# Inverse of the delta rule's triangles: 32x32 and 64x64 tiles in the doubling steps, and a semaphore of its own for each scratch load

## The reference, cut to what matters

```python
lmat = jnp.where(strict, jnp.einsum('bhncd,bhnsd->bhncs', k_beta, k) * decay, 0.0)
tmat = lax.linalg.triangular_solve(eye + lmat, eye, left_side=True, lower=True)
u_c = jnp.einsum('bhncs,bhnsd->bhncd', tmat, v_beta)
```

## Time and profile before

| | |
|---|---|
| median of 3 runs | 2074.65 us (2069.03 to 2075.73) |
| the profiled execution | 2070.47 us |
| its span, first to last instruction | 2068.9 us |
| TensorE busy | 98% |
| VectorE, ScalarE, GpSimd busy | 45%, 36%, 4% |
| mean granted clock of TensorE | 0.991 |

### The profile page before, as it was taken

One profiled execution on the slowest core, in us unless ns is written; L12 is line 12 of the kernel. 1 busy time (PEld: TensorE's weight loads), 2 busy tenths in 40 slices (PEclk: granted clock), 3 DMA queues, 4 the chain that ended last, 5 costly groups with the idle time before them and its releaser, 6 DMA issues.

```text
span 2068.9 us, 33700 instructions
## 1 busy us (share of the span) xinstructions
PE 2021.4 (98%) x12540; PEld 1806.5 (87%) x12540; DVE 922.9 (45%) x2325; ACT 738.9 (36%) x2211; POOL 90.6 (4%) x115
## 2 busy tenths in 40 slices
PE   5999999999999999999999999999999999999996
PEld 5888899999999999999999988888888888888885
DVE  6333344556455455545556454322223534344332
ACT  5422224235252433525335252423224322223333
POOL 4000000000000000000000000000000000000000
PEclk8999999999999999999999999999999999999998
DMA  6133332234133241332323233343345444345222
GB/s 222 43 106 110 114 126 90 68 103 117 41 114 85 83 116 53 104 92 95 97 83 100 78 111 87 113 134 115 106 134 206 138 132 132 120 143 204 87 76 81
DMA packets 229516, 225.55 MB, mean 109 GB/s; under 512 B 33681, under 2 KB 214890, under 8 KB 228746
## 3 DMA queue, kind: packets, MB, share of 16 engines
q1 hardware_dynamic: 167090, 180.10, 27.0%
q10 hardware_dynamic: 55944, 22.63, 4.4%
q0 software_dynamic: 6368, 21.14, 3.1%
HBM read 199.65 MB, written 25.30 MB: 109 GB/s over the span
## 4 chain that ended last, share of the span: by engine, by line
PE 93%; DMA 3%; DVE 1%; ACT 1%; issue 1%; ACTq 0%; POOL 0%; SPq 0%; DVEq 0%
PE pj L518 80%; PE pg L518 10%; DMA st<-inverse_scratch 3%; PE pt L518 2%; PE pt L665 1%; PE pg L761 0%; PE pg L818 0%; DVE fst L1235 0%; POOL xl L1708 0%; ACTq L996 0%; DMA prow<-in_dn_norm_w 0%; ACT wh L859 0%; DVE res L1688 0%; DVE xl L1241 0%; ACTq L995 0%
## 5 line engine op out<-in xcount | busy, mean ns | idle before, releaser
L518 PE MATMUL pj<-xh,wh 128*128 128x264 f32 (+2 forms) x2688 | 739.2, 329 | 3.0 <-DVE wl L1210 3.0
L518 PE MATMUL pj<-xl,wh 128*128 128x264 f32 (+2 forms) x2688 | 719.8, 322 | 0.0
L518 PE MATMUL pj<-xh,wl 128*128 128x264 f32 (+2 forms) x2688 | 718.2, 322 | 0.0
L1210 DVE TENSOR_TENSOR wl<-raw,wh 128x256 fp32r<-128x256 f32 x896 | 346.3, 424 | 609.6 <-ACT wh L859 607.8
L518 PEld LDWEIGHTS pj<-xh,wh 128*128 128x128 f32 x2688 | 448.3, 190 | 46.9 <-issue 3.6
L518 PEld LDWEIGHTS pj<-xh,wl 128*128 128x128 f32 x2688 | 448.4, 190 | 38.0
L518 PEld LDWEIGHTS pj<-xl,wh 128*128 128x128 f32 x2688 | 448.2, 189 | 37.5 <-issue 1.0
L859 ACT ACTIVATE wh<-raw 128x256 fp32r<-128x256 f32 x896 | 306.3, 407 | 63.0 <-issue 42.7
L859 ACT ACTIVATE wh<-rawb 128x256 fp32r<-128x256 f32 x288 | 97.8, 406 | 182.2 <-PE pj L518 181.2
L518 PE MATMUL pj<-yl,wh 128*128 128x512 f32 x384 | 149.5, 389 | 0.0
L518 PE MATMUL pj<-yh,wl 128*128 128x512 f32 x384 | 149.5, 389 | 0.0
(11 more groups left out here) (210 smaller groups left out, 1719.5 us busy)
## 6 DMA issues: line engine op xcount, KB each, us to landing
raw<-in_w_in SPq DMA_DIRECT2D x112, 1024.0 KB, 6.3
rawb<-in_w_dn_out SPq DMA_DIRECT2D x16, 1024.0 KB, 6.1
rawb<-in_w_o SPq DMA_DIRECT2D x12, 1024.0 KB, 5.4
gates_scratch<-stg ACTq DMA_DIRECT2D x32, 256.0 KB, 2.1
rawb<-in_w_pool_out SPq DMA_DIRECT2D x8, 1024.0 KB, 5.5
gst<-gates_scratch POOLq DMA_DIRECT2D x32, 256.0 KB, 3.1
yraw<-branch_scratch SPq DMA_DIRECT2D x1, 5632.0 KB, 22.7
xt<-in_x SPq DMA_DIRECT2D x4, 1024.0 KB, 6.9
```

Of the source, the lines that this page charges most:

```text
L518: return pe.matmul(dst, lhs, rhs, start=start, stop=stop)
L1210: tt(wl[:, j, 2 * q:2 * q + 2, :], raw[:, 2 * par + h, 2 * q:2 * q + 2, c * P:(c + 1) * P], wh[:, j, 2 * q:2 * q + 2, :].bitcast(F32), ALU ...
```

## The change

The two lower levels no longer load whole slots. At L0 every 32x32 block on the diagonal of `mk` is its own product with the 16 columns of `tm` that belong to its upper half, written to the same 32 partitions: 4 for each slot. At L0+1 T takes three such products for each slot and comes first, Y takes four with 16 columns of weights. The second level uses 32x32 tiles (two for each slot in X and Y, one in T), and L0+4 a 64x64 tile. The masks are gone: X of the first level is scaled by a column `odd` that is 1 on rows 16 to 31 of each 32 and 0 elsewhere, the second level is copied from the right partitions. `xm`, `xm5` and `xm6` are three parts of `dec` that don't overlap, and nothing clears them. Where a block was zero, VectorE writes the negated product instead of subtracting. `tm` and the two loads of `st` get a semaphore each, and L0+1 waits for `st`. Four steps get an `alone()`.

```diff
@@ the column that replaces the masks
-    for i, size in enumerate((BS, 2 * BS)):
...
+    c[:, CODD] = s // BS % 2
@@ views of dec
-        xm = dec
+        xm = dec[:, 0:SLOTS * BS].rearrange("p (i c) -> p i c", c=BS)
+        xm5 = dec[:, 128:128 + SLOTS * 2 * BS].rearrange("p (i c) -> p i c", c=2 * BS)
+        xm6 = dec[:, 384:384 + SLOTS * LOWC].rearrange("p (i c) -> p i c", c=LOWC)
+        QUARTERS = [slice(32 * b, 32 * b + 32) for b in range(4)]
+        PAIRED = [(QUARTERS[0], QUARTERS[1]), (QUARTERS[2], QUARTERS[3])]
@@ TensorE
                 if m == L0:
-                    wait(inv_loaded, 48, 48)
-                    pe.wait_ge(masks_loaded, 16)
+                    wait(tm_loaded, 16, 16)
                     wait(qk_ready, 2, 2)
                     alone()
                     for i in range(SLOTS):
-                        mm = product(pg[0][:, LOWC * i:LOWC * (i + 1)].rearrange("p (b c) -> p b c", c=BS),
-                                     slot(mk, i), halves(slot(tm, i), BS, 0), True, True)
+                        for q in QUARTERS:
+                            mm = product(pg[0][q, BS * i:BS * (i + 1)], slot(mk, i)[q, q], slot(tm, i)[q, q.start:q.start + BS], True, True)
                     mm.then_inc(x_mm, 1)
                 if m == L0 + 1:
-                    wait(x_ready, 3, 1)
+                    wait(st_loaded, 32, 32)
+                    wait(x_ready, 4, 1)
+                    alone()
...
+                        for q in QUARTERS[0:3]:
+                            mm = product(pg[2][q, BS * i:BS * (i + 1)], slot(st, i)[q, q], xm[q, i, :], True, True)
+                    mm.then_inc(t_mm, 1)
...
+                        for q in QUARTERS:
+                            mm = product(pg[1][q.start:q.start + BS, BS * i:BS * (i + 1)], xm[q, i, :], slot(st, i)[q, q.start + BS:q.stop],
+                                         True, True)
                     mm.then_inc(y_mm, 1)
                 if m == L0 + 2:
                     wait(t_ready, 2, 1)
+                    alone()
...
+                        for first, second in PAIRED:
+                            mm = product(pg[0][second, 2 * BS * i:2 * BS * (i + 1)], slot(mk, i)[first, second], slot(tm, i)[first, first],
+                                         True, True)
                 if m == L0 + 3:
...
+                        mm = product(pg[2][second, 2 * BS * i:2 * BS * (i + 1)], slot(st, i)[second, second], xm5[second, i, :], True, True)
...
+                            mm = product(pg[1][first, 2 * BS * i:2 * BS * (i + 1)], xm5[second, i, :], slot(st, i)[second, second], True, True)
                 if m == L0 + 4:
...
-                        mm = product(pg[0][:, LOWC * i:LOWC * (i + 1)], slot(mk, i), slot(tm, i)[:, 0:LOWC], True, True)
+                        mm = product(pg[0][LOWC:P, LOWC * i:LOWC * (i + 1)], slot(mk, i)[0:LOWC, LOWC:P], slot(tm, i)[0:LOWC, 0:LOWC], True, True)
@@ ScalarE
-                    act.dma_start(slots(tm), full_rows(inv_d[1])).then_inc(inv_loaded, 16)
-                    act.dma_start(slots(st), full_rows(inv_d[0])).then_inc(inv_loaded, 16)
+                    act.dma_start(slots(tm), full_rows(inv_d[1])).then_inc(tm_loaded, 16)
+                    act.dma_start(slots(st), full_rows(inv_d[0])).then_inc(st_loaded, 16)
@@ VectorE
-                        dve.wait_ge(masks_loaded, 16)
-                        wait(xm_zeroed, 1, 1)
-                    tt(each(xm, BS << lv, 0), low(pg[0]).rearrange("p i (b c) -> p i b c", c=BS << lv), mask(lv), ALU.mult).then_inc(x_ready, 1)
+                if m == L0:
+                    wait(x_mm, 3, 1)
+                    dve.tensor_scalar(xm, by_slot(pg[0], BS), odd, None, ALU.mult).then_inc(x_ready, 1)
                 if m == L0 + 1:
                     wait(t_mm, 2, 1)
...
+                    for q in QUARTERS[0:3]:
+                        part = slots(tm)[q, :, q.start:q.start + BS]
+                        ins = tt(part, part, by_slot(pg[2], BS)[q], ALU.subtract)
+                    ins.then_inc(t_ready, 1)
+                    wait(y_mm, 3, 1)
+                    for q in QUARTERS:
...
+                if m == L0 + 2:
+                    wait(x_mm, 3, 2)
+                    for first, second in PAIRED:
+                        dve.tensor_copy(xm5[second], by_slot(pg[0], 2 * BS)[second]).then_inc(x_ready, 1)
@@ GpSimd
-            pool.dma_start(lvm[:, :, :], consts[:, CLEV:CZERO].rearrange("p (l c) -> p l c", l=2)).then_inc(masks_loaded, 16)
-                pool.wait_ge(qk_ready, 2 * d + 2)
-                pool.sem_inc(pool_gate, 1)
-                pool.memset(xm[:, 0:XC], 0.0).then_inc(xm_zeroed, 1)
```

More of the change, by code:

```diff
@@ L691, in delta @@
                     mm.then_inc(x_mm, 1)
                 if m == L0 + 3:
-                    wait(x_ready, 3, 2)
+                    wait(x_ready, 4, 3)
                     wait(s_ready, 3, 1)
+                    alone()
+                    first, second = PAIRED[0]
                     for i in range(SLOTS):
-                        mm = product(pg[1][:, LOWC * i:LOWC * (i + 1)].rearrange("p (b c) -> p b c", c=2 * BS),
-                                     slot(xm, i), halves(slot(st, i), 2 * BS, 1), True, True)
+                        mm = product(pg[2][second, 2 * BS * i:2 * BS * (i + 1)], slot(st, i)[second, second], xm5[second, i, :], True, True)
@@ L698, in delta @@
+                    mm.then_inc(t_mm, 1)
+                    for i in range(SLOTS):
+                        for first, second in PAIRED:
+                            mm = product(pg[1][first, 2 * BS * i:2 * BS * (i + 1)], xm5[second, i, :], slot(st, i)[second, second], True, True)
                     mm.then_inc(y_mm, 1)
-                    for i in range(SLOTS):
-                        mm = product(pg[2][:, 2 * BS * i:2 * BS * (i + 1)], slot(st, i), slot(xm, i)[:, 0:2 * BS], True, True)
-                    mm.then_inc(t_mm, 1)
@@ L1443, in delta @@
                         dve.tensor_copy(wtr, wblk.rearrange("p a i -> p i a")).then_inc(w_turned, 1)
[L1445 to L1451, removed]
-                    return lvm[:, level, :].unsqueeze(1).broadcast_to([P, SLOTS, LOWC]).rearrange("p i (b c) -> p i b c", c=BS << level)
@@ L1467, in delta @@
+                if m == L0 + 2:
+                    wait(x_mm, 3, 2)
+                    for first, second in PAIRED:
+                        dve.tensor_copy(xm5[second], by_slot(pg[0], 2 * BS)[second]).then_inc(x_ready, 1)
                 if m == L0 + 3:
                     wait(t_mm, 2, 2)
-                    part = slots(tm)[32:64, :, 0:32]
-                    tt(part, part, pg[2][32:64, 0:32 * SLOTS].rearrange("p (i c) -> p i c", c=32), ALU.subtract).then_inc(t_ready, 1)
-                    for b in range(2):
-                        rows = slice(64 * b, 64 * b + 32)
-                        part = slots(st)[rows, :, 64 * b + 32:64 * b + 64]
-                        ins = tt(part, part, low(pg[1])[rows, :, 32 * b:32 * b + 32], ALU.subtract)
+                    first, second = PAIRED[0]
+                    part = slots(tm)[second, :, first]
+                    dve.tensor_scalar(part, by_slot(pg[2], 2 * BS)[second], -1.0, None, ALU.mult).then_inc(t_ready, 1)
+                    wait(y_mm, 3, 2)
+                    for first, second in PAIRED:
+                        part = slots(st)[first, :, second]
+                        ins = dve.tensor_scalar(part, by_slot(pg[1], 2 * BS)[first], -1.0, None, ALU.mult)
@@ L1483, in delta @@
                     wait(y_mm, 3, 3)
[L1484 to L1485 removed]
+                    dve.tensor_scalar(slots(st)[0:LOWC, :, LOWC:P], by_slot(pg[1], LOWC)[0:LOWC], -1.0, None, ALU.mult).then_inc(s_ready, 1)
                 if R0 <= m < O0:
```

54 lines of the change are left out of this document (19 added, 35 removed).

## The result

The changed kernel takes **2000.62 us** (median of 4 runs, 2000.11 to 2001.15), against 2071.84 for the kernel before in the same comparison: ratio 0.9657, 95% interval 0.9641 to 0.9673. Its profiled execution took 2000.11 us, 70.4 less than the one of before. I had forecast 2062 with a range from 2030 to 2086, so the forecast failed, and on the cautious side: the time lies nearest to the rival of the tiles that work side by side (1985).

What follows compares the result with a forecast made beforehand. The prediction took TensorE, busy 98%, to bound the kernel: 2070.5 - 9.4 (wait at L0) - 1 (units and shapes) + 0 (clock) = 2060 us, forecast as 2062 for a median, range 2030 to 2086.

Steps and rivals of the forecast that it cites:

- the rival of the tiles that work side by side: Rival for the five steps of the inverse: four units share one time, -74 us, giving 1985 us; chance 0.05.
- What bounds the kernel, and the wait at L0: TensorE, busy 98%, sets the end; L0 waiting for `tm` alone removes its gap in each pair, -9.4 us.
- The number of units: L0 to L0+4: more but smaller two-multiply units, 53 ns each once ready ones run out; sum -0.82 us a pair.
- the array's pace: Rival: units run at 31 ns for 32 columns and 25 for 16 throughout, giving 2034 us; chance 0.20.
- A sum of -0.1 us a pair: Units and changes of tile shape together in the inverse's steps, -1 us in all.
- Changes of shape: Switching tile shape around the bursts of the inverse costs 0.2 us in and out, +0.7 us a pair.
- VectorE: Its changed updates and copies cost nothing; uncovered, a late answer at L0+1 or L0+3 costs up to 1 us a pair.
- The clock: Falls of TensorE's granted clock in most pairs around L0+1, net 0 us, with -4.6 and +8 as the ends.
- Slower at 60 ns a unit: Rival: small-tile units cost 60 ns, +13 us, and the clock stays low, giving 2093 us; chance 0.14.

Runs made afterwards that it cites:

- the second run: The changed kernel with the wait for `st` moved from L0+1 back to L0, so only the small tiles are left: 2007.9 us.
- 5: The changed kernel with L0 as two products a slot on the two diagonal 64x64 tiles, half of the first level's blocks left out: 1997.8 us.

## Why the prediction was wrong, point by point

- **What bounds the kernel, and the wait at L0.** Right. TensorE sets the end, L0 now starts 0.2 us behind the projection, and the gaps gave 8.6 us in the profile and 7.2 in the comparison with the second run, where I had 9.4. Nothing came late in its place.
- **The number of units: the step that failed.** I had the array's pace right (31 ns for 32 columns, 25 for 16, measured 31.9 and 24.9 on one tile), and then laid a slower limit over it: "I read this as some 27 ns an instruction, and take 53 ns a unit". The two starts 30 ns apart in the earlier trace rows are the delay of one multiply behind its weight load when the engine has stood still, a latency; I took it for the interval between any two instructions. The 64x64 burst, which I called the only long one, runs at 61 ns because that is the pace of 64 columns of weights on one tile (29 ns a unit with two tiles at work), not because nothing comes faster. In the changed kernel a unit, two instructions, starts every 8.7 ns. A limit of supply does exist, but it is 27 ns a unit and shows only once the stock is used up; in the changed kernel it cost 5.6 us, as holes and not as a spacing. The other half of the failure was to give 0.05 to tiles side by side. "No row speaks for it" was true, but no row spoke against it either, since no burst of before used two tiles; the Trainium skill, TensorEngine Tiling (Array Packing), section Key Properties, states that different tiles work in parallel, and the experiments with the order turned and with one tile show it. A silence of the trace deserved the range between the two, not one end.
- **What this cost step by step.** L0 2.64 forecast, 0.66 measured; L0+1 5.18 and 1.15; L0+2 0.99 and some 0.4 without the tails (0.96 less 0.59 for them); L0+3 1.79 and 1.03. L0+4, 64x64 tiles on one place, was right: -0.84 forecast, -0.75 measured (1.82 to 1.07). A sum of -0.1 us a pair became -7.7 without the holes.
- **The rival that came nearest.** 1985 assumed that four units share one time in every step. They do at L0 and in Y of L0+1. At L0+4 all units lie on one tile, in T of L0+3 too, and in X of L0+2 on two: 2.5 us a pair were forecast for the five steps, which took some 4.3 (0.66, 1.15, 0.4, 1.03 and 1.07), the change of shape in them. The rest is the holes, which no case of mine had.
- **Changes of shape.** 0.09 us into a burst (0.21 instead of 0.12 from the last projection multiply) and 0.11 behind it: the 0.2 of the prediction holds for a change of shape. Going from tile to tile inside a burst costs nothing that shows: the 8.7 ns have a new tile at every product.
- **VectorE.** Costed at nothing, and in these steps TensorE doesn't wait for it: the profile has no wait of TensorE for `dec`, `tm` or `st`, though the updates take longer (seven small ones instead of two at L0+1).
- **The clock.** "I expect falls in most pairs" was wrong: none. Of the -4.6 to +8 us that I allowed, the lower end came true. The runs show falls behind long stretches in which little of the array works (one tile, seven pairs of eight) and behind holes of 2.5 us, and none where four tiles work without such a hole; what exactly decides stays open, for the order turned gave bursts of 1.8 and 2.7 us without a fall.
- **Slower at 60 ns a unit.** The figure of 62 ns for each multiply, which the Trainium skill, TensorE: Matmul & The Clock Gate, section Wait — 56ns, not 53.3ns?, gives for decoding in software, is not what this trace shows: 8.7 ns a unit, and 31.9 on one tile.

## What to carry to other kernels

Small products, each on its own part of the array, overlap if neighbours in the queue lie on different tiles: loop over the tiles inside and over the batch outside, and mix steps that lie on different tiles. On one tile a unit costs what its weight columns cost (here 25, 32, 60 and 111 ns for 16, 32, 64 and 128), so count the units of the busiest tile, not all of them. Once such bursts are short, look at the supply of instructions: here 128 units in less than 3.5 us outran it. Fewer products can cost less than the hole (2.9 us gained in 5, in a single run that leaves out blocks); more long multiplies between the bursts might do the same, which no run tried.

## What the runs showed of the hardware that I had not expected

- Units on four tiles start 8.7 ns apart on average; all four write to the same accumulator tensor `pg0`, in different partitions. Four times 8.7 is 35 ns a unit on each tile, against 31.9 where one tile works alone, so they hardly slow each other.
- Tiles in the same rows overlap as well: X of L0+2 with the tails, T with Y of L0+3 (0.63 us for 48 units that took 1.03 in two groups).
- Instructions arrive in blocks of 256, and a block is usable some 3.5 us after the one before it when they are used at full speed. The place of a hole depends on the number of instructions ahead in the program, even at its very start: 32 more moved it by 16 units, 68 more by 68 instructions.
- A semaphore instruction in a row of them costs some 0.15 us of TensorE's issue, 17 times a unit in a burst: 32 of them held the engine up for 2.5 us after what was queued had run out.
- A hole or a burst on one tile costs a second time, since the granted clock falls behind it: 1.2 us for each block of 12 projection multiplies (2.88 against 1.64).
